# A hybrid attention and mixture-of-experts step on one core: experts chosen by ranks, the first job's tokens formed by one-hot products

## Chip, core and metric

The kernel runs on one core of a Trainium2 chip. The metric is the time of the whole program on the device, in microseconds (us); lower is better. A core has TensorE (PE, matrix products into eight PSUM banks), VectorE (DVE), ScalarE (ACT), GpSimd (POOL) and SyncE (SP), which here only issues DMAs. Engines meet by semaphores.

## What is computed

One layer over 512 prompt tokens and 64 sampled tokens (8 sequences of 8), width 1024, in fp32: attention in three branches and a pooling mixer, then `h = x + [a, m] @ w_out`, and on `rmsnorm(h)` a hierarchical mixture of 16 experts in 4 groups of 4. Each token takes its best group, and in it the two best experts:

```python
pg = softmax(x @ w_router_group)            # the best of 4 groups
g_val, g_idx = top_k(pg, 1)
le = (x @ w_router_expert)[experts of group g_idx]
e_val, e_idx = top_k(softmax(le), 2)
gate = g_val * e_val / sum(e_val)
y += gate_e * ((silu(x @ w_gate[e]) * (x @ w_up[e])) @ w_down[e])
```

The output is `h + y`, with the new key and value rows and pooling states beside it.

## The kernel before

The program is written by hand, engine by engine, in one block; each engine runs its list in order. The 576 tokens lie in five tiles, four of 128 rows and a last one of 64 (`ROWS`), and the residual `h` stays in `xh`. The stages are: input projection, compression of the cached keys, attention of the prompt, attention of the samples, and from about 366 us the output projection and the router.

**Router.** For each tile DVE adds the projection to `xh`, ACT sums the squares, DVE computes the inverse root `rstd` and writes `n2`, the normed row times `norm2_g` with its columns regrouped by eights (`by_chunk`), and ACT stores `n2` to `normed_rows` in HBM (`n_stored`). PE turns `xh` (L1265), DVE multiplies by `g2` (L2097), PE makes the logits (L1274), DVE scales them (L2117). For the last tile the normed row comes before the logits are read. Then DVE picks the group and two experts by a chain of maxima, comparisons and priorities (L2127 to L2153), each step waiting for the one before (`link`). PE counts with triangular matrices how many tokens before each one chose the same expert (`prefix`, L1313 and L1315). DVE derives for each token and choice a `job` and a `row` in it (L2164 to L2174) and writes one-hot matrices `picks` (L2182). PE turns them into `idx` (L1323), the token in each row of each job, and DVE copies it (L2190). Where PE would stand still, `keep_clock(k)` issues `WARM[k]` products whose result nobody reads (L1281, L1283).

**Jobs.** The experts' work is cut into `NJ` = 12 jobs of 128 rows: 96 rows of one expert, 32 of the fourth of its group of experts. POOL gathers the 128 token rows of a job from `normed_rows` by `idx` into `xg` (L2424), two buffers deep. PE turns them (L1337, `gathered_T`), ACT and DVE copy the halves into `xgT` (L1636, L2229), and PE runs gate, up and down products (L1353, `trio`) with 32-column stationary pieces. The transposes of job j+1 stand between the up and the down products of job j. Rows of a finished job go to HBM, those of the last are spread by a one-hot product. At the end rows are gathered, weighted and added. `crowded` reads `nmax`, the largest number of tokens of an expert, into a register of each engine, for a branch that is not taken here.

**Loads.** SP loads the 48 expert matrices of 2 MB into eight slots, in order; each load waits for the product that last used its slot (L836). The eighth goes over the buffers `n2`, and waits until all tiles are stored.

Of the kernel before, what the change touches and what calls it, by code (L numbers as in the profile page):

```python
# [42 lines left out]
WARM = (1, 2, 7, 3, 6)  # L43
# [123 lines left out]
def psum_plan():  # L167
# [103 lines left out]
    add("idx")  # L271
    add(("warm", 4))
# [3 lines left out]
def hybrid_step(nc, a, out, scratch):  # L276

    with ExitStack() as ctx:
# [91 lines left out]
        g2 = sb("g2", [P, KC])  # L370
        xnT = amT
# [93 lines left out]
        r16 = [view(kTs, 100 + i * 80, TILES, NE) for i in range(5)]  # L465
# [9 lines left out]
        in_fourth, base, late, job, row, beyond, which = (view(kTw, 330 + i * 10, 2, TILES) for i in range(7))  # L475
        r4 = [view(kTw, 400 + i * 20, TILES, NG) for i in range(4)]
# [22 lines left out]
        xg = [view(pflat, i * D, D) for i in range(2)]  # L499
        xgT = view(pflat, 2 * D, KC, P)  # L500
# [145 lines left out]
        def _(sp):  # L646
# [32 lines left out]
            sp.dma_start(g2[:, :], a["norm2_g"].rearrange("(k p) -> p k", p=P), allow_slow_non_contiguous=True).then_inc(ld_c1, 16)  # L679
            sp.dma_start(slc_bias[:, :], a["c_bands"]).then_inc(ld_c2, 16)  # L680
# [157 lines left out]
            for n, (e, m, _) in enumerate(matrix_loads()):  # L838
# [35 lines left out]
        def _(pe):  # L874
# [481 lines left out]
            def trio(j):  # L1356

                pe.wait_ge(xgt_ready, j * 2 + 2)
# [15 lines left out]
                for half in range(2):  # L1374
                    if j + 1 < NJ:
                        gathered_T((j + 1) % 2, (j + 1) // 2 * 16 + 16, [half])
# [5 lines left out]
                if j:  # L1382
                    pe.wait_ge(y_taken, j * 2)
                for half in range(2):
# [8 lines left out]
            gathered_T(0, 16, [0, 1])  # L1393
# [4 lines left out]
            pe.wait_ge(xgt_ready, 2 * NJ)  # L1398
# [51 lines left out]
        def _(sc):  # L1450
# [160 lines left out]
            for i in range(TILES):  # L1611
# [13 lines left out]
                sc.wait_ge(n_ready, i + 1)  # L1625
                sc.dma_start(scratch["n2"][i * P:i * P + n, :], n2[i % 2][0:n, :]).then_inc(n_stored[i % 2], 16)
# [11 lines left out]
            def trio(j):  # L1638
# [5 lines left out]
                if j + 1 < NJ:  # L1644
                    gathered(j + 2)
# [10 lines left out]
            gathered(1)  # L1656
# [23 lines left out]
        def _(ve):  # L1680
# [398 lines left out]
            link(ve.memset(logits, 0.0))  # L2079
            for i in range(TILES):  # L2080
# [19 lines left out]
                def normed_rows():  # L2100
# [3 lines left out]
                    link(ve.reciprocal(rstd[0:n, 1, i:i + 1], st[0:n, 16 + i:17 + i]))  # L2104
                    if i == 0:
                        ve.wait_ge(ld_g2, 16)
                    if i >= 2:
                        ve.wait_ge(n_stored[i % 2], 16 * (i // 2))
                    by_chunk = lambda row: row.rearrange("p (q k) -> p k q", k=KC)
                    ve.scalar_tensor_tensor(n2[i % 2][0:n, :].rearrange("p (k q) -> p k q", k=KC), by_chunk(xh[0:n, i, :]),  # L2110
# [3 lines left out]
                for stage in ((normed_rows, rows_of_router) if i < TILES - 1 else (rows_of_router, normed_rows)):  # L2114
                    stage()
# [11 lines left out]
            link(ve.tensor_reduce(r1[0], lg, X, ALU.max))  # L2127
            link(ve.tensor_tensor(r4[0], lg, over4(r1[0]), ALU.subtract))
            link(ve.tensor_tensor(r4[2], lg, over4(r1[0]), ALU.is_equal))
            link(ve.tensor_tensor(r4[2], r4[2], wide("prio4", NG), ALU.mult))  # L2130
            link(ve.tensor_reduce(r1[3], r4[2], X, ALU.max))
            link(ve.tensor_tensor(r4[3], r4[2], over4(r1[3]), ALU.is_equal))
            link(ve.tensor_scalar(r4[2], r4[3], -NEG, NEG, ALU.mult, ALU.add))
            ge = lambda x: x.rearrange("p t (g e) -> p t g e", g=NG)
            pen = spread(r4[2].rearrange("p t (g a) -> p t g a", a=1), 3, EPG)
# [455 lines left out]
```

## Time and profile before

| | us |
|---|---|
| median of 3 runs | 752.14 (752.06 to 753.49) |
| the profiled execution, its time | 753.13 |
| its span, first to last instruction | 751.4 |
| PE busy | 712.4 (95%) |
| DVE busy | 268.7 (36%) |
| ACT busy | 170.1 (23%) |
| POOL busy | 231.6 (31%) |

The span is what the trace's clock shows; the profiled execution's own time lies 1.73 us above it. Busy shares are means over stages with different limits, so the stretch around the router has to be read in the timeline.

### The profile page before, as it was taken

What the parts mean: (1) busy time and instruction counts of PE and PEld (TensorE: products, weight loads), DVE (VectorE), ACT (ScalarE), POOL (GpSimd) and SP (SyncE); (2) the same over time, 40 slices, a digit from 0 to 9 for tenths busy, and PEclk for the clock granted to TensorE, in tenths of its full rate; (3) what the DMA queues carried; (4) which work ended last, traced back from release to release, by engine and by line L of the source; (5) the groups of instructions that cost most, each with busy time, mean ns of one, the idle gap of its engine ahead of it and who ended that gap; (6) DMA issues with size and microseconds to landing.
All of it is one profiled execution on the core that took longest, in us unless ns stands there. A gap on an engine that the chain in (4) does not pass through costs nothing.

```text
span 751.4 us, 16367 instructions
## 1 busy us (share of the span) xinstructions
PE 712.4 (95%) x6460; PEld 401.1 (53%) x6460; DVE 268.7 (36%) x724; ACT 170.1 (23%) x366; POOL 231.6 (31%) x393
## 2 busy tenths in 40 slices
PE   6999999999989887988999998999999999999998
PEld 3555456865766554666645544454445555445542
DVE  1200054068678768566222366110011110001147
ACT  3100030248456644333010121000101000110100
POOL 2465156898575647444000001000000000000050
PEclk9999999999999899999999999999999999999999
DMA  9966523069801998467995065699999999999874
GB/s 300 262 174 230 173 50 71 20 198 226 228 20 40 323 310 266 134 180 211 241 415 223 29 265 182 241 321 358 399 419 425 419 422 420 424 413 420 352 270 137
DMA packets 81938, 191.79 MB, mean 255 GB/s; under 512 B 15798, under 2 KB 54982, under 8 KB 77373
## 3 DMA queue, kind: packets, MB, share of 16 engines
q1 hardware_dynamic: 67461, 150.63, 56.0%
q0 software_dynamic: 12160, 31.97, 13.0%
q10 hardware_dynamic: 2240, 8.13, 2.7%
q8 instruction: 52, 0.85, 0.4%
q14 instruction: 25, 0.20, 0.1%
HBM read 174.09 MB, written 16.70 MB: 254 GB/s over the span
## 4 chain that ended last, share of the span: by engine, by line
PE 53%; DVE 8%; issue 3%; DMA 2%; ACT 1%; SPq 1%; POOL 0%; DVEq 0%; POOLq 0%; ACTq 0%
PE bank L1353 31%; PE bank L1254 7%; PE bank L1337 2%; DVE arena L2011 2%; PE bank L1200 1%; PE bank L1445 1%; PE bank L1283 1%; PE bank L1274 1%; PE bank L1245 1%; DMA arena<-in_w_out 1%; DMA arena<-expert_rows,row_i 1%; DVE arena L2021 1%; DVE arena L2014 1%; PE bank L1379 1%; PE bank L1106 1%
## 5 line engine op out<-in xcount | busy, mean ns | idle before, releaser
L1353 PE MATMUL bank<-arena,proj 128*32 128x256 f32 (+1 forms) x2352 | 237.0, 479 | 1.3 <-DVE proj L2229 0.8
L1353 PEld LDWEIGHTS bank<-arena,proj 128*32 128x32 f32 x2352 | 103.3, 110 | 94.7 <-issue 76.3
L2424 POOL DMA_INDIRECT proj<-normed_rows,idx x12 | 11.4, 953 | 302.6 <-PE bank L1337 190.7
L909 PE MATMUL bank<-arena,amT 128*128 128x454 f32 x256 | 101.8, 556 | 1.1 <-DMA arena<-in_w_in 1.1
L2239 DVE TENSOR_TENSOR proj<-proj,bank 128x256 f32<-128x256 f32 x24 | 10.0, 421 | 208.1 <-PE bank L1353 208.1
L2334 POOL DMA_DIRECT2D arena<-in_cache_cmp_kv x128 | 68.6, 536 | 50.3 <-issue 42.6
L909 PEld LDWEIGHTS bank<-arena,amT 128*128 128x128 f32 x256 | 48.9, 194 | 50.0 <-issue 49.9
L2341 POOL DMA_DIRECT2D arena<-in_cache_slc_kv x96 | 51.5, 536 | 42.0 <-PE bank L1203 17.7
L1353 PE MATMUL bank<-amT,proj 128*32 128x512 f32 (+1 forms) x336 | 56.5, 532 | 0.0
L1353 PE MATMUL bank<-queries_and_bias,proj 128*32 128x512 f32 (+1 forms) x384 | 56.5, 486 | 0.0
L2354 POOL COPY arena<-arena 128x268 f32<-128x268 f32 x64 | 37.8, 647 | 27.9 <-PE bank L906 20.3
L1520 ACT ACTIVATE arena<-arena,st 128x512 f32<-128x512 f32 (+3 forms) x48 | 26.6, 554 | 35.5 <-DVE st L1915 35.5
L1650 ACT ACTIVATE proj<-bank 128x512 f32<-128x512 f32 x24 | 14.3, 598 | 82.5 <-PE bank L1353 82.5
L1353 PEld LDWEIGHTS bank<-queries_and_bias,proj 128*32 128x32 f32 x384 | 21.4, 110 | 17.3 <-issue 13.7
L1353 PEld LDWEIGHTS bank<-amT,proj 128*32 128x32 f32 x336 | 19.4, 110 | 19.1 <-issue 17.4
L1254 PE MATMUL bank<-arena,amT 128*128 128x512 f32 x64 | 29.0, 596 | 0.1
L1636 ACT ACTIVATE proj<-bank 128x512 f32<-128x512 f32 x12 | 7.2, 597 | 96.8 <-PE bank L1337 96.8
L1915 DVE CUSTOM_DVE_ANT_0 arena<-bank,queries_and_bias 128x512 f32<-128x512 f32 (+3 forms) x48 | 21.6, 488 | 13.3 <-PE bank L1063 12.4
L2435 POOL DMA_INDIRECT arena<-expert_rows,row_i x8 | 8.0, 998 | 56.9 <-DMA expert_rows<-proj 54.8
L1643 ACT ACTIVATE proj<-bank 128x512 f32<-128x512 f32 x12 | 7.2, 598 | 77.4 <-PE bank L1353 77.4
L1106 PE MATMUL bank<-mats,arena 128*128 128x128 f32 x120 | 19.4, 296 | 4.6 <-ACT proj L1535 4.4
L2354 POOL COPY xh<-arena 128x268 f32<-128x268 f32 x32 | 22.5, 749 | 4.0 <-PE bank L926 3.9
(358 smaller groups left out, 1011.9 us busy)
## 6 DMA issues: line engine op xcount, KB each, us to landing
arena<-in_w_up SPq DMA_DIRECT2D x13, 2048.0 KB, 16.5
arena<-in_w_down SPq DMA_DIRECT2D x13, 2048.0 KB, 16.6
arena<-in_w_gate SPq DMA_DIRECT2D x10, 2048.0 KB, 17.1
arena<-in_cache_cmp_kv POOLq DMA_DIRECT2D x128, 64.0 KB, 2.5
arena<-in_cache_cmp_kv SPq DMA_DIRECT2D x128, 64.0 KB, 2.2
amT<-in_w_gate SPq DMA_DIRECT2D x3, 2048.0 KB, 12.8
queries_and_bias<-in_w_gate SPq DMA_DIRECT2D x3, 2048.0 KB, 11.6
expert_rows<-proj ACTq DMA_DIRECT2D x11, 512.0 KB, 9.7
```

The source lines that it names most:

```text
L909: last = pe.matmul(ps(("in", c, i))[0:n, 0:WC], xnT[:, k, i * P:i * P + n], w_in[c % 2][:, k, :], start=k == 0, stop=k == KC - 1)
L1106: last = pe.transpose(ps(("p_T", u, k))[:, c * P:(c + 1) * P], pS[u % 4][:, k, c * P:(c + 1) * P], ident)
L1254: last = pe.matmul(ps(("h", i, half))[0:n, :], amT[:, k, i * P:i * P + n], out_matrix(k, half), start=k == 0, stop=k == KC - 1)
L1337: last = pe.transpose(BX[half][:, k * P:(k + 1) * P], xg[slot][:, c:c + P], ident)
L1353: ins = pe.matmul(dst[part, :], rows[:, part], own if q < TRIO else shared, start=start, stop=stop)
L1520: sc.activation(z, z, ACT.Exp, bias=st[:, m:m + 1], scale=-1.0, accum_out=st[:, d:d + 1]).then_inc(p_e, 1)
L1650: sc.activation(ytok[:, half * 512:(half + 1) * 512], BY[half][:, :], ACT.Copy).then_inc(y_taken, 1)
L1915: read(ve.tensor_tensor_reduce(pS[u % 4][:, k, 0:n], ps(("p_s", u, k))[:, 0:n], dist[:, SEQ - n:SEQ], -SLOPES[g + G * k], 3e38, ALU.add, A ...
L2011: read(ve.scalar_tensor_tensor(z3, lanes, table["row_slope"], ps(name)[:, :].rearrange("p (n l) -> p n l", l=64), ALU.mult, ALU.add), name)
L2334: po.dma_start(sides[:, b // 4, b % 4 * PAGES + k, :], src).then_inc(ld_last, 16)
L2341: po.dma_start(pages[b % 4][:, k, first * P:(first + count) * P], src)\
L2354: po.tensor_copy(chunk_out(r, d), chunk_in(d)).then_inc(regrouped, 1)
```

## The change

Three things change. First, the experts are chosen by ranks: within the groups, and within each group of four experts, every value is compared with every other (`beats4`, `beats16`; an earlier one wins a tie), the comparisons are summed to ranks, and ranks 0 and 1 of the group of rank 0 are the choice. The maxima that the gates need are taken later. Second, the rows of job 0 are not fetched. DVE writes for each tile `spot`, a one-hot matrix from token to row of job 0, scaled by `rstd`, and PE multiplies `xh` (read by `by_chunk`, stationary) with it; the result is the turned rows in two banks, and ACT and DVE multiply by `g2_rows` (a new load of `norm2_g`) into `xgT`. POOL fetches jobs 1 to 11. Third, the normed rows of the last tile are written after `idx`, into `xg[0]`, and stored later. `WARM` is shorter.

```diff
-WARM = (1, 2, 7, 3, 6)
+WARM = (1, 2, 4, 2)
...
+    for half in range(2):
+        add(("rows", half), bank=2 + half)
+    add("idx", bank=5)
...
+        def normed(i):
+
+            return n2[i % 2] if i < TILES - 1 else xg[0]
...
+            sp.dma_start(g2_rows[:, :], a["norm2_g"].rearrange("(p k) -> p k", p=P)).then_inc(ld_c1, 16)
...
-                    sp.wait_ge(n_stored[0], 48)
+                    sp.wait_ge(n_stored[0], 32)
...
+            for half in range(2):
+                opened(pe, ("rows", half))
+            for i in range(TILES):
+                n = ROWS[i]
+                pe.wait_ge(picks_ready, i + 1)
+                by_chunk = xh[0:n, i, :].rearrange("p (q k) -> p k q", k=KC)
+                for half in range(2):
+                    for k in range(4):
+                        last = pe.matmul(ps(("rows", half))[:, k * P:(k + 1) * P], by_chunk[:, 4 * half + k, :], spot[0:n, i, :],
+                                         start=i == k == 0, stop=i == TILES - 1 and k == 3)
+                    if i == TILES - 1:
+                        written(last, ("rows", half))
             opened(pe, "idx")
             for n in range(2 * TILES):
                 i, k = n // 2, n % 2
-                pe.wait_ge(picks_ready, n + 1)
+                pe.wait_ge(picks_ready, TILES + n + 1)
                 last = pe.matmul(ps("idx")[:, 0:NJ], picks[:, n, :], tok_at[:, k, i, :], start=n == 0, stop=n == 2 * TILES - 1)
             written(last, "idx")
-            keep_clock(4)
...
-                pe.wait_ge(free[b], used[b])
+                if b != plan["idx"][0]:
+                    pe.wait_ge(free[b], used[b])
...
-                pe.wait_ge(xgt_ready, j * 2 + 2)
+                if j:
+                    pe.wait_ge(xgt_ready, 2 * j)
...
-            gathered_T(0, 16, [0, 1])
...
+                if i < TILES - 1:
+                    sc.wait_ge(n_ready, i + 1)
+                    sc.dma_start(scratch["n2"][i * P:i * P + n, :], normed(i)[0:n, :]).then_inc(n_stored[i % 2], 16)
+            filled(sc, ("rows", 0))
+            for k in range(4):
+                last = sc.activation(xgT[:, k, :], ps(("rows", 0))[:, k * P:(k + 1) * P], ACT.Copy, scale=g2_rows[:, k:k + 1])
+            read(last, ("rows", 0))
+            sc.wait_ge(n_ready, TILES)
+            sc.dma_start(scratch["n2"][SEQ:NT, :], normed(TILES - 1)[0:NS, :]).then_inc(n_stored[0], 16)
...
+            link(ve.memset(rstd[:, 1, :], 0.0))
...
+                if i < TILES - 1:
+                    inverse_root()
+                    normed_rows(i)
+                    rows_of_router()
+                else:
+                    rows_of_router()
+                    inverse_root()
...
+            link(ve.memset(chosen[:, TILES, :], 0.0))
...
+            groups = lg.rearrange("p t (a g) -> p t a g", a=1)
+            experts = ge(le)
+
+            for j in range(NG):
+                for low, high, better in ((0, j + 1, ALU.is_gt), (j + 1, NG, ALU.is_ge)):
+                    if low < high:
+                        one = spread(groups[:, :, :, j:j + 1], 3, high - low)
+                        ve.tensor_tensor(beats4[:, :, low:high, j], one[:, :, 0, :], lg[:, :, low:high], better)
+                        one = spread(experts[:, :, :, j:j + 1], 3, high - low)
+                        last = ve.tensor_tensor(beats16.rearrange("p (t g) i j -> p t g i j", g=NG)[:, :, :, low:high, j], one,
+                                                experts[:, :, :, low:high], better)
+            link(last)
+            ve.tensor_reduce(rank4, beats4, X, ALU.add)
+            link(ve.tensor_reduce(rank16.rearrange("p t (g e) -> p (t g) e", g=NG), beats16, X, ALU.add))
+            link(ve.scalar_tensor_tensor(in_group, rank4, 0.0, over4(table["valid"]), ALU.is_equal, ALU.mult))
+            its_group = spread(in_group.rearrange("p t (g a) -> p t g a", a=1), 3, EPG)
+            ve.scalar_tensor_tensor(ge(chosen[:, 0:TILES, :]), ge(rank16), 1.5, its_group, ALU.is_lt, ALU.mult).then_inc(oh_ready, 1)
+            for k in range(2):
+                last = ve.scalar_tensor_tensor(ge(hot[:, k]), ge(rank16), float(k), its_group, ALU.is_equal, ALU.mult)
+            link(last)
...
+            roots = spread(rstd[:, 1, :].rearrange("p (a i) -> p a i", a=1), 1, 2)
+            link(ve.scalar_tensor_tensor(in_first, job, 0.0, roots, ALU.is_equal, ALU.mult))
+            for i in range(TILES):
+                for k in range(2):
+                    last = ve.tensor_scalar((spot[:, i, :], picks[:, i, :])[k], table["row"], row[:, k, i:i + 1], in_first[:, k, i:i + 1],
+                                            ALU.is_equal, ALU.mult)
+                link(last)
+                ve.tensor_tensor(spot[:, i, :], spot[:, i, :], picks[:, i, :], ALU.add).then_inc(picks_ready, 1)
...
+            ve.wait_ge(picks_ready, TILES)
...
+            filled(ve, ("rows", 1))
+            read(ve.tensor_tensor(xgT[:, 4:8, :], ps(("rows", 1))[:, :].rearrange("p (k t) -> p k t", k=4), bc(g2_rows[:, 4:8], P), ALU.mult),
+                 ("rows", 1))
...
+            normed_rows(TILES - 1)
+
+            link(ve.tensor_reduce(r1[0], lg, X, ALU.max))
+            link(ve.tensor_tensor(r4[0], lg, over4(r1[0]), ALU.subtract))
+            link(ve.tensor_tensor(pair16, hot, over_k(le), ALU.mult))
+            link(ve.tensor_reduce(top, pair16, X, ALU.add))
+            ve.tensor_tensor(r1[6], top[:, 1, :], top[:, 0, :], ALU.subtract).then_inc(r_exp_in, 1)
...
-            gathered(1)
...
-            for j in range(NJ):
-                if j >= 2:
-                    po.wait_ge(xt_full, j - 1)
+            for j in range(1, NJ):
+                if j >= 3:
+                    po.wait_ge(xt_full, j - 2)
```

In the same diff, the counts of `gathered`, `gathered_T`, `xt_full` and `xgt_ready` are lowered by one job, job 0's down products wait for `idx` to be copied, and the old selection (L2127 to L2154, `first_max`) is deleted.

On PE, between the last logits and job 0, before (`mats` as the only source is filler, `kTw,mats` the counting, `proj` with 12 columns is `idx`, `mats,proj` the transposes of fetched rows):

```order
L1283 MATMUL bank<-mats 128x512 x7
L1313 MATMUL bank<-kTw,mats 128x96
...
L1281 MATMUL bank<-mats 128x128
L1283 MATMUL bank<-mats 128x512 x3
L1323 MATMUL bank<-proj 128x12 x10
L1281 MATMUL bank<-mats 128x128
L1283 MATMUL bank<-mats 128x512 x6
L640 TENSOR_LOAD nmax
L640 ISA x2
L1337 MATMUL bank<-mats,proj 128x128 x8
L1353 MATMUL bank<-arena,proj 32x512 x32
```

And after:

```order
L1297 MATMUL bank<-mats 128x512 x4
L1327 MATMUL bank<-kTw,mats 128x96
...
L1295 MATMUL bank<-mats 128x128
L1297 MATMUL bank<-mats 128x512 x2
L1341 MATMUL bank<-proj,xh 128x128 x40
L1349 MATMUL bank<-proj 128x12 x10
L653 TENSOR_LOAD nmax
L653 ISA x2
L1379 MATMUL bank<-arena,proj 32x512 x32
```

The forty products stand between the shortened filler and `idx`; the filler behind `idx` and the eight transposes are gone, and the register read follows `idx`.

On DVE, from the end of `row` to behind the copy of `idx`, before (`kTw` holds the small values, `proj` the one-hots):

```order
L2174 SCALAR_TENSOR_TENSOR kTw<-kTw 128x10
L2176 TENSOR_TENSOR proj<-small,kTw 128x120
L2178 TENSOR_TENSOR proj<-proj,small 128x60 x2
L2182 TENSOR_SCALAR proj<-small,kTw 128x128 x10
L2184 TENSOR_REDUCE kTw<-bank 128x1
L2186 CAST nmax<-kTw 1x1
L2189 COPY kTw<-bank 128x1
L2190 CAST idx<-bank 128x12
L2194 TENSOR_TENSOR kTw<-kTs,small 128x160
```

And after (L2148 is the line of `normed_rows`):

```order
L2211 SCALAR_TENSOR_TENSOR kTw<-kTw,rstd 128x10
L2214 TENSOR_SCALAR proj<-small,kTw 128x128 x2
L2217 TENSOR_TENSOR proj<-proj 128x128
...
L2221 TENSOR_TENSOR proj<-proj,small 128x60 x2
L2226 TENSOR_SCALAR proj<-small,kTw 128x128 x10
L2228 TENSOR_REDUCE kTw<-bank 128x1
L2230 CAST nmax<-kTw 1x1
L2233 TENSOR_TENSOR proj<-bank,g_rows 128x512
L2236 COPY kTw<-bank 128x1
L2237 CAST idx<-bank 128x12
L2148 SCALAR_TENSOR_TENSOR proj<-xh,rstd,proj 64x1024
L2242 TENSOR_REDUCE kTw<-kTs 128x5
```

The scaled one-hots of five tiles come ahead of everything that serves `idx`, the copy out of the `rows` bank ahead of the copy of `idx`, and the normed rows of the last tile behind it.

## Rows read from the trace of the kernel before

**Rows 1.** Chain that ended last, expert jobs: start us, us, what.

```profile
467.34 13.98 PE bank L1353 x192
...
482.78 20.80 PE bank L1353 x256
```

**Rows 2.** Waits of SP's DMA queue: total us, times, longest.

```profile
SPq L836 <- PE bank L1353: 230.7, 31, 23.9
```

**Rows 3.** The same chain, just before job 0.

```profile
459.35 5.15 PE bank L1283 x12
464.51 0.96 issue
465.46 1.10 PE bank L1337 x8
```

**Rows 4.** Timeline around the selection: start us, us, engine, line, operation, names, count.

```profile
444.40 2.07 DVE L2110 SCALAR_TENSOR_TENSOR queries_and_bias<-xh,rstd,proj 64x1024 f32<-64x1024 f32 x1
...
445.16 6.17 PE L1283 MATMUL bank<-mats 128*128 128x512 f32 x14
...
446.39 0.22 DVE L2117 TENSOR_SCALAR kTs<-bank,rstd 64x20 f32<-64x20 f32 x1
...
446.74 0.18 DVE L2127 TENSOR_REDUCE kTw<-kTs 128x5 f32<-128x20 f32 x1
...
451.93 0.24 DVE L2153 TENSOR_TENSOR kTw<-kTw,small 128x80 f32<-128x80 f32 x1
```

**Rows 5.** Timeline from the counting products to the end of DVE's list.

```profile
452.23 0.46 PE L1313 MATMUL bank<-kTw,mats 128*128 128x96 f32 x2 [0.89 <-DVE kTw L2153]
...
453.85 0.32 DVE L2164 TENSOR_TENSOR kTw<-kTs,bank 128x160 f32<-128x160 f32 x1 [0.24 <-PE bank L1315]
...
454.56 0.17 DVE L2167 TENSOR_SCALAR kTw<-kTw 128x10 f32<-128x10 f32 x1
...
454.64 0.17 DVE L2168 TENSOR_SCALAR kTw<-kTw 128x10 f32<-128x10 f32 x1
...
455.49 0.16 DVE L2174 SCALAR_TENSOR_TENSOR kTw<-kTw 128x10 f32<-128x10 f32 x1
...
456.39 2.05 DVE L2182 TENSOR_SCALAR proj<-small,kTw 128x128 f32<-128x128 f32 x10
...
456.82 2.37 PE L1323 MATMUL bank<-proj 128*128 128x12 f32 x20 [0.35 <-DVE proj L2182]
...
459.43 0.17 DVE L2190 CAST idx<-bank 128x12 int32<-128x12 f32 x1
...
465.19 0.23 DVE L2222 TENSOR_SCALAR kTw<-small,kTw 128x5 f32<-128x5 f32 x1
```

**Rows 6.** Timeline of PE in the pooling products of 128 x 128 by 128 columns.

```profile
130.31 0.39 PE L945 MATMUL bank<-queries_and_bias,proj 128*128 128x128 f32 x2
130.54 0.39 PE L947 MATMUL bank<-queries_and_bias,proj 128*128 128x128 f32 x2
```

**Rows 7.** Groups of DVE instructions by shape: busy us, mean ns.

```profile
L1975 DVE COPY xh<-arena 128x268 f32<-128x268 f32 x16 | 10.7, 708 | 1.2 <-POOL arena L2359 1.1
...
L1967 DVE COPY proj<-bank 128x512 f32<-128x512 f32 x9 | 6.1, 685 | 0.6 <-PE bank L1106 0.6
...
L2266 DVE TENSOR_SCALAR proj<-small,kTw 128x128 f32<-128x128 f32 x5 | 1.4, 346 | 0.0
```

**Rows 8.** DMA issues, 440 to 470 us: KB, us to landing; then all twelve fetches.

```profile
normed_rows<-queries_and_bias ACTq DMA_DIRECT2D x1, 256.0 KB, 3.7
proj<-normed_rows,idx POOLq DMA_INDIRECT x3, 4.4
...
DMA to landing us min/median/max: 4.3/8.5/11.1
```

**Rows 9.** Page, section 5: busy us, mean ns, idle before.

```profile
L909 PE MATMUL bank<-arena,amT 128*128 128x454 f32 x256 | 101.8, 556 | 1.1 <-DMA arena<-in_w_in 1.1
```

**Rows 10.** Windows: us, busy us (count) of PE, PEld, DVE, ACT, POOL, clock, DMA share, GB/s.

```profile
450.00:456.00 6.00, 5.11 (x23) 2.73 (x21) 5.08 (x26) 0.32 (x2) 0.00 (x0) 1.00 0.80 279
```

More of the change, by code:

```diff
@@ L370, in hybrid_step @@
         g2 = sb("g2", [P, KC])
+        g2_rows = sb("g2_rows", [P, KC])
         xnT = amT
@@ L464, in hybrid_step @@
         w_r = sb("w_r", [P, KC, NG + NE])
-        r16 = [view(kTs, 100 + i * 80, TILES, NE) for i in range(5)]
+        rank16 = view(kTs, 100, TILES, NE)
+        hot = view(kTs, 100 + 2 * 80, 2, TILES * NE).rearrange("p k (i e) -> p k i e", e=NE)
+        beats16 = view(QB[:, :, :].rearrange("p a b -> p (a b)"), 0, TILES * NG, EPG, EPG)
+        beats4 = view(QB[:, :, :].rearrange("p a b -> p (a b)"), TILES * NE * EPG, TILES, NG, NG)
+        rank4, in_group = (view(kTs, 500 + i * 20, TILES, NG) for i in range(2))
+        top = view(kTs, 540, 2, TILES)
         pair16 = view(kTw, 96, 2, TILES * NE).rearrange("p k (i e) -> p k i e", e=NE)
@@ L475, in hybrid_step @@
         in_fourth, base, late, job, row, beyond, which = (view(kTw, 330 + i * 10, 2, TILES) for i in range(7))
+        in_first = view(kTw, 510, 2, TILES)
         r4 = [view(kTw, 400 + i * 20, TILES, NG) for i in range(4)]
@@ L1375, in trio @@
                     if j + 1 < NJ:
-                        gathered_T((j + 1) % 2, (j + 1) // 2 * 16 + 16, [half])
+                        gathered_T((j + 1) % 2, (j + 2) // 2 * 16, [half])
                     pe.wait_ge(he_ready, 2 * j + half + 1)
@@ L1383, in trio @@
                     pe.wait_ge(y_taken, j * 2)
+                else:
+                    taken(pe, "idx")
                 for half in range(2):
@@ L1644, in trio @@
                 if j + 1 < NJ:
-                    gathered(j + 2)
+                    gathered(j + 1)
                 if j:
@@ L2098, in rows_of_router, with inverse_root @@
                              ("nT", i, half))
-                def normed_rows():
+                def inverse_root():
                     ve.wait_ge(h_sq, i + 1)
@@ L2126, in _ @@
             wide = lambda name, n: spread(table[name].rearrange("p (a n) -> p a n", a=1), 1, TILES)
[L2127 to L2132, printed above, removed]
@@ L2145, in _ @@
-            flat = lambda x: x.rearrange("p a b -> p (a b)")
-            first_max(r16[0], r1[4], r16[2])
-            link(ve.scalar_tensor_tensor(flat(r16[1]), flat(r16[2]), NEG, flat(r16[0]), ALU.mult, ALU.add))
-            first_max(r16[1], r1[6], r16[3])
-            hot = view(kTs, 100 + 2 * 80, 2, TILES * NE).rearrange("p k (i e) -> p k i e", e=NE)
-            link(ve.memset(chosen[:, TILES, :], 0.0))
-            link(ve.tensor_tensor(chosen[:, 0:TILES, :], r16[2], r16[3], ALU.add))
@@ L2153, in _ @@
-            ve.tensor_tensor(chosen[:, 0:TILES, :], chosen[:, 0:TILES, :], over16(table["valid"]), ALU.mult).then_inc(oh_ready, 1)
-            ve.tensor_tensor(r1[6], r1[6], r1[4], ALU.subtract).then_inc(r_exp_in, 1)
+            link(ve.memset(chosen[:, TILES, :], 0.0))
+            ge = lambda x: x.rearrange("p t (g e) -> p t g e", g=NG)
+            groups = lg.rearrange("p t (a g) -> p t a g", a=1)
[8 more added lines that the diff above has]
+                                                experts[:, :, :, low:high], better)
@@ L2155, in _ @@
+            for k in range(2):
+                last = ve.scalar_tensor_tensor(ge(hot[:, k]), ge(rank16), float(k), its_group, ALU.is_equal, ALU.mult)
+            link(last)
             over_k = lambda x: spread(x.rearrange("p (a i) e -> p a i e", a=1), 1, 2)
-            link(ve.tensor_tensor(hot, hot, over_k(over16(table["valid"])), ALU.mult))
             link(ve.tensor_tensor(pair16, hot, over_k(wide("seat", NE)), ALU.mult))
@@ L2247, in trio @@
                 if j + 1 < NJ:
-                    gathered(j + 2)
+                    gathered(j + 1)
             def gathered_rows(i):
@@ L2476, in _ @@
             po.wait_ge(st_pool, 16 * (1 + DB))
-N_C1 = 16 * (1 + 3 + 2 + 4 + 2 + 1 + 1)
+N_C1 = 16 * (1 + 3 + 2 + 4 + 2 + 1 + 2)
 N_OUT = 3 + 3 + DB
```

27 lines of the change are left out of this document (7 added, 20 removed).

## The prediction

> **What bounds the kernel now.** I read the page first (TensorE, PE, is busy 95% of the span), then the chain of work that ended last, the waits of the DMA queue, and the timeline around the router. From 467.34 us on, twelve expert jobs run on PE: the gate and up products of job 0 take 13.98 us, and each later piece of 20.8 us is followed by 1.5 us of transposes, 22.33 us a job, with no gap that a transfer causes [rows 1]. The loads of expert matrices wait for PE's products, 230.7 us in all, so the weights follow PE and not the other way round [rows 2]. Whatever moves the start of job 0 (call it S, 467.34 now) moves the end by as much, as long as nothing in job 0 starts to wait. The prediction is therefore about S.
>
> Before S stands a serial stretch. VectorE (DVE) picks experts, PE counts them, DVE makes one-hot matrices, PE turns these into `idx`, GpSimd (POOL) fetches rows, PE transposes them. At its end PE is not waiting for the fetch: it runs its own filler products until 464.50, then 0.96 us of its queue reading `nmax` into a register, then the transposes [rows 3], 1.9 us up to S with their copies.
>
> **The router on DVE.** Now `normed_rows` of the last tile (2.07 us) stands between DVE and the last logits, though PE had ended them at 445.1: they are read at 446.39 [rows 4]. After the change they are read at about 445.1, a gain of 1.3 us. The selection starts 0.35 us after that read and its one-hots are ready at 452.17, so it takes 5.4 us [rows 4]. The new one is 14 comparisons that do not wait for one another, then two sums, and two products. Unlinked small operations start 0.08 us apart [rows 5], and one of 128 elements takes 0.205 us of the pace (ten in 2.05 us) [rows 5], so about 0.07 us plus 1.05 ns per element. 14 x 0.07 + 400 elements x 1.05 ns = 1.4 us, the wait behind them 0.1, the clearing of `chosen` 0.1, the sums 0.15 and 0.5 (320 elements), the products 0.2 and 0.25: 2.7 us. The one-hots are ready at 445.1 + 0.35 + 2.7 = 448.2, 4.0 us earlier. PE's filler before it is cut from 7 to 4 products. Seven took 6.17 us [rows 4], 0.86 each, so four end at 448.7. The filler now ends last by 0.4 us, and hides an error of that size in the 2.7. The counting products start at 448.6 instead of 452.23; DVE reads them 1.62 us later, at 450.2, and has `row` and `job` at 452.0 (455.65 now, from 453.85 + 1.80) [rows 5]. Up to here 3.6 us are gained.
>
> **Job 0 without a fetch.** DVE adds `in_first` (0.2 us), then for each tile two scaled one-hots and their sum. The scaled one-hot exists now, in another place: 0.346 us each [rows 7], at a pace like that of the plain ones. Per tile 0.2 + 0.35 + 0.03 for the link + 0.28 for the sum, of which the next tile hides a little: 0.85 us, the first ready at 453.2. PE then multiplies: 5 tiles x 8 chunks, 40 products of 128 x 128 with 128 columns, two records each. The nearest rows are the pool products of the same shape: one starts each 0.2225 us (130.31 to 130.54) [rows 6]. 40 x 0.2225 = 8.9 us, so PE sets the pace (1.78 us per tile against 0.85 on DVE), and the `rows` banks are full at 453.2 + 8.9 + 0.2 = 462.3. Behind them in PE's order stand the ten `idx` products, 2.37 us [rows 5]; they end at 464.5. DVE's one-hots for these (2.05 us [rows 5], and 0.75 us for `tok_at`) are done near 459.3 and `nmax` near 459.9, behind PE. The copies out of the `rows` banks take 0.69 us on DVE [rows 7] and about 1 us on ScalarE (ACT), whose half is full 0.9 us earlier; both are over at 463.1, under the `idx` products. The 6 filler products, the 8 transposes and their 0.70 us copy are gone. What is left is the register read: 0.96 us now, when PE's last product must have ended first. After the change it follows `idx` directly and waits only for the copies, so it costs between 0 (read while the products drain) and 0.96. I take half: S = 464.5 + 0.5 = 465.0, 2.3 us earlier than 467.34. The gain of 3.6 us shrinks because the path from `row` to S grows from 11.7 to 13.0 us.
>
> **What is late next.** Every one of POOL's fetches now waits for the last tile's store, and that is written later: `idx` is read at 464.9 on DVE, `normed_rows` ends at 467.0, ACT issues the store, which lands after 3.7 us at 470.7, and POOL issues job 1's fetch at 471.0. It lands after 4.4 us with idle queues: 475.4 [rows 8]. PE asks for it when job 0's up products are done, S + 13.98 = 479.0. The cover is 3.6 us; with the median landing of all fetches, 8.5 us, it is gone and 0.5 us over [rows 8]. Behind `normed_rows` DVE has five new operations (1.2 us) and its old list, 459.60 to 465.42 now [rows 5], done at about 474.0, and a register read like PE's, 475.0; its first hidden product is due at S + 10.5 = 475.5. Close, but PE needs that product only after S + 14. ACT's exponentials with their table load fit before the first Silu at S + 7. The load of `w_up` into `queries_and_bias` no longer waits for the last store; it was not waited for.
>
> **At nothing:** the extra small load of `g2_rows` moves SyncE's later issues by one issue. The input products waited for a load for 1.1 us in all, once, at their first, ahead of this issue [rows 9]; page loads run far ahead of their use. Clearing `rstd` falls into DVE's wait for the first projection.
>
> **Sum** on the profiled execution: span 751.4 - 2.3 = 749.1, its time 753.13 - 2.3 = 750.8. The median of the three runs is 0.99 us under that profiled time, 752.14 - 2.3 = **749.8 us**. Its own range is 748.9 to 751.0 (the register read at either end, 0.4 us on the comparisons). A measurement of this kernel can tell about 0.2%, 1.5 us, from no change.
>
> **Rival 1: the stationary operand is read with gaps (slower).** `by_chunk` takes every eighth float of `xh`, 32 bytes apart, and no PE row before does that. DVE has such rows: 268 elements read with gaps take 708 ns, and 512 read densely out of a bank 685 ns [rows 7], so an element costs twice, about 2.1 ns. If PE's weight loads double their pace of 0.111 us, 80 of them cost 8.9 us more and the time is 758.7. If they cost DVE's 2.1 ns for each of 128 columns, 0.267 us each, it is 12.5 us more, 762.3. It decides from 2.3 us on, that is at 0.14 us per load. Against it speaks only that the loads overlap the streams (two in flight) and that another engine's reads set no price for PE. I give it 0.31, two thirds of that at the doubled pace.
>
> [...]
>
> **Rival 2: job 1's tokens come late.** With the slowest landing, 11.1 us [rows 8], the fetch is there at 482.1, PE waits 3.1 us in job 0 and the time is 752.9; with 8.5 us it is 750.3. For it: job 1's load of the down matrix starts at S + 7 and shares the queues. Against it: only one such load is then under way. 0.12, at about 751.5.
>
> **Rival 3: the new DVE work gains nothing.** If each of the 14 comparisons costs what a linked one does (0.24 us), they take 3.4 us instead of 1.4, beyond the filler's cover of 0.4: 1.6 us, and with slower scaled one-hots 2.3 us, 752.1. 0.08.
>
> [...] 0.04 for this and the unforeseen.
>
> **Numbers.** Forecast 0.45, rival 1 0.31, rival 2 0.12, rival 3 0.08, rest 0.04. Faster: 0.45 + half of rival 2 + a little = 0.52; same 0.14; slower 0.34. The range must take in the doubled pace of rival 1, and leaves out its upper price: 748.9 to 759.3.
>
> **What would show it.** In the changed profile: the last logits read near 445.1; the one-hots 3 us later; forty products at L1341 in 8.9 us (17.8 or more under rival 1, with weight loads clearly over 0.19 us each); job 0's first product at 465.0; PE's wait for job 1's transposes at about 479 at most some tenths; jobs still 22.33 us apart. The prediction is wrong if the forty products take over 11 us, or if PE waits for the fetch.

## The result, and the profile after

The change made the kernel slower: 764.77 us (764.3 to 767.76, 4 runs) against 752.82 us (752.06 to 755.21, 4 runs) of the kernel before beside it, a ratio of 1.0174 [1.0154, 1.0193]. The forecast was 749.8, with 759.3 as its upper end. The profiled execution took 764.3 us, with a span of 762.6. Everything ahead of the change's place ran 1.6 us earlier in this execution than in the one of before (the last logits end at 443.46, not 445.07), so times around the router are compared below as distances from that end, called L.

The chain of work that ended last, in the changed kernel: start us, us, what.

```profile
443.72 3.44 PE bank L1297 x8
...
447.35 1.06 PE bank L1329 x10
...
451.62 19.59 PE bank L1341 x80
471.21 4.38 PE bank L1349 x20
475.58 16.51 PE bank L1379 x192
...
493.56 20.80 PE bank L1379 x256
...
515.84 20.85 PE bank L1379 x256
```

The reader is to see the forty products (80 records) at 19.59 us, the `idx` products at 4.38 instead of 2.37 [rows 5], and job 0's first piece at 16.51 instead of 13.98 [rows 1]. Job 0 starts at L + 32.1 (before L + 22.3). Behind it the jobs are 22.33 us apart as before.

DVE's timeline in the same execution (start us, us, engine, line, operation, names, shapes, count, idle before):

```profile
443.57 0.23 DVE L2160 TENSOR_SCALAR kTs<-bank,rstd 64x20 f32<-64x20 f32 x1 [0.82 <-PE bank L1288]
...
445.35 0.30 DVE L2181 TENSOR_TENSOR QB<-kTs 128x80 f32<-128x80 f32 x1
...
446.56 0.24 DVE L2188 SCALAR_TENSOR_TENSOR kTw<-kTs 128x80 f32<-128x80 f32 x1
...
450.54 0.60 DVE L2214 TENSOR_SCALAR proj<-small,kTw 128x128 f32<-128x128 f32 x2
451.18 0.29 DVE L2217 TENSOR_TENSOR proj<-proj 128x128 f32<-128x128 f32 x1
451.39 0.60 DVE L2214 TENSOR_SCALAR proj<-small,kTw 128x128 f32<-128x128 f32 x2
```

The logits are read 0.1 us after L, the one-hots are ready at 446.80, L + 3.3 (predicted 3.1), and a tile's scaled one-hots take 0.85 us (predicted 0.85). The first of the forty products starts at L + 8.2 (predicted 8.1). All terms up to there held.

What a single one of the forty costs: the instructions of line L1341 in the changed kernel, their duration in ns (min/median/max).

```profile
L1341 PEld LDWEIGHTS bank<-proj,xh x80: 309/335/340, 451.6 to 470.6; 128*128 128x128 f32 x64, 64*128 64x128 f32 x16
L1341 PE MATMUL bank<-proj,xh x80: 364/402/502, 451.6 to 470.8; 128*128 128x128 f32 x64, 64*128 64x128 f32 x16
```

And the windows of the changed kernel (columns as in [rows 10]; the clock is the third number from the end):

```profile
453.00:454.00 1.00, 1.00 (x6) 1.00 (x6) 0.97 (x5) 0.00 (x0) 0.00 (x0) 0.75 0.09 16
454.00:455.00 1.00, 1.00 (x6) 1.00 (x6) 0.97 (x4) 0.00 (x0) 0.00 (x0) 0.50 0.00 0
...
457.00:458.00 1.00, 1.00 (x6) 1.00 (x5) 0.73 (x5) 0.00 (x0) 0.00 (x0) 1.00 0.00 0
...
462.00:468.00 6.00, 6.00 (x26) 5.88 (x26) 0.00 (x0) 0.00 (x0) 0.00 (x0) 1.00 0.00 0
...
474.00:480.00 6.00, 6.00 (x32) 2.67 (x35) 4.02 (x10) 1.19 (x1) 0.00 (x0) 0.50 0.10 23
```

The clock was not at 1.00 throughout this stretch, as it was before (1.00 from 444 to 486 us): it was at 0.50 from 453.5 to 456.9 and again from 470.6 to 480.8. In what follows such a stretch is called a spell. Each window counts every record that touches it, so that six in one microsecond are about four that start in it; the 6 us at 462 show 26. A weight load starts every 0.24 us in the first spell and every 0.24 us behind it, so their pace did not follow the clock. In the second spell `idx` (4.38 us for 2.37) and job 0 (16.51 for 13.98) did slow down.

### The profile page after: what moved, and what is told of

Read it like the earlier page. It is cut to its first block, busy times and chain, and to the rows that moved or that the text cites. A ratio compares the mean times of both kernels' runs of the same rounds, so it can differ in the third digit from the quotient of the medians.

```text
span 762.6 us, 16494 instructions
## 1 busy us (share of the span) xinstructions
PE 725.3 (95%) x6511; PEld 416.7 (55%) x6511; DVE 271.4 (36%) x743; ACT 170.7 (22%) x369; POOL 230.3 (30%) x392
## 4 chain that ended last, share of the span: by engine, by line
PE 58%; DVE 6%; issue 2%; ACT 1%; DVEq 0%; ACTq 0%
PE bank L1379 33%; PE bank L1268 7%; PE bank L1341 3%; PE bank L1214 2%; DVE arena L2045 1%; PE bank L1363 1%; PE bank L1473 1%; PE bank L1288 1%; PE bank L1259 1%; DVE arena L2055 1%; PE bank L1297 1%; DVE arena L2048 1%; PE bank L1406 1%; PE bank L1090 1%; PE bank L1120 1%
## 5 line engine op out<-in xcount | busy, mean ns | idle before, releaser
L1379 PE MATMUL bank<-arena,proj 128*32 128x256 f32 (+1 forms) x2352 | 239.6, 484 | 0.2
L1379 PE MATMUL bank<-amT,proj 128*32 128x512 f32 (+1 forms) x336 | 58.2, 537 | 0.0
L1379 PE MATMUL bank<-queries_and_bias,proj 128*32 128x512 f32 (+1 forms) x384 | 58.2, 501 | 0.0
## 6 DMA issues: line engine op xcount, KB each, us to landing
arena<-in_w_up SPq DMA_DIRECT2D x13, 2048.0 KB, 17.6
```

Source lines behind the costliest of these rows:

```text
L1379: ins = pe.matmul(dst[part, :], rows[:, part], own if q < TRIO else shared, start=start, stop=stop)
```

## The experiments

Theory A was rival 1: the stationary operand read 32 bytes apart sets the pace of the products. Theory B: the clock sets it. Experiments 1, 2, 5 and 6 ran on one chip, beside 752.24 us of the kernel before (19 runs); L is taken anew from each profile.

**1. Dense columns (r1_dense).** Features of job 0 are mixed up by it.

```diff
-                by_chunk = xh[0:n, i, :].rearrange("p (q k) -> p k q", k=KC)
+                by_chunk = xh[0:n, i, :].rearrange("p (k q) -> p k q", k=KC)
```

> The changed kernel, but the forty products for job 0 read their stationary operand densely (128 neighbouring columns of the residual) instead of every eighth. This mixes up the order of job 0's input features, so its output is not the reference's; sizes and counts are the same. Theory A (the gaps in the stationary read make each weight load slow, and the clock falls because PE then computes too little): forty products in 8.9 us instead of 19.6, clock 1.00 throughout, idx products 2.4 us instead of 4.4, job 0's gate and up 14.0 us instead of 16.5; 15.1 us less than 764.8, so 749.7 us. Theory B (the clock falls because filler products were taken out, and the slow products are a result of that): the products stay above 15 us, the clock still falls, the time stays above 758 us.

Measured: 753.83 us (10 runs), ratio 1.0015 [0.9996, 1.0034], span 751.0. Its chain, the instructions of L1341, and windows:

```profile
452.81 9.36 PE bank L1341 x80
462.18 2.33 PE bank L1349 x20
464.51 15.61 PE bank L1379 x192
```

```profile
L1341 PEld LDWEIGHTS bank<-proj,xh x80: 183/192/192, 452.8 to 461.8; 128*128 128x128 f32 x64, 64*128 64x128 f32 x16
```

```profile
463.00:464.00 1.00, 1.00 (x11) 1.00 (x11) 0.00 (x0) 0.00 (x0) 0.00 (x0) 1.00 0.00 0
...
465.00:466.00 1.00, 1.00 (x12) 0.36 (x8) 0.94 (x1) 0.00 (x0) 0.00 (x0) 0.50 0.00 0
```

That one word is worth 10.2 us of products and 143 ns of each weight load. Job 0 starts at 464.51, L + 19.85 (predicted 19.9), with some luck: even dense, the products take 9.36 us and not 8.9, and the register read, put at 0.5, costs nothing. Yet the kernel is no faster than before. The clock falls to 0.50 at 464.8 for 3.4 us, and job 0's first piece takes 15.61 us instead of 13.98. Of the gain of 2.4 us that leaves 0.8, and in the profiled execution the last stage took just that back: a store of experts' rows and the fetch behind it took 3.79 + 6.03 us, against 2.62 + 6.40 before. These terms put the ratio at 0.9989 without the last stage and at 1.000 with it; what the median has beyond that isn't explained. Theory A holds for the products; its "job 0 14.0" failed.

**2. A ladder of steps (r2_ladder).** Tile 0 is read with step 1, tiles 1 to 4 with 2, 3, 4 and 8 floats (so other features).

```diff
+                step = (1, 2, 3, 4, 8)[i]
+                by_chunk = [xh[0:n, i, c:c + step * (P - 1) + 1:step] for c in range(KC)]
...
```

> The changed kernel, but the five tiles of the forty products read the stationary operand with steps of 1, 2, 3, 4 and 8 elements (4, 8, 12, 16, 32 bytes), 16 records each; the output is not the reference's, since other columns of the residual are read. [...] Theory A, in a form where any gap costs: 0.24 us from step 2 on. Theory B: all five tiles alike, at the pace that the clock sets.

Measured: 761.23 us (one run), products 14.56 us. Weight loads of the five tiles, from windows inside each, in tile order:

```profile
L1342 PEld LDWEIGHTS bank<-proj,xh x16: 186/192/192, 452.9 to 454.5; 128*128 128x128 f32 x16
...
L1342 PEld LDWEIGHTS bank<-proj,xh x15: 192/197/198, 454.5 to 456.2; 128*128 128x128 f32 x15
...
L1342 PEld LDWEIGHTS bank<-proj,xh x15: 198/261/264, 456.3 to 458.6; 128*128 128x128 f32 x15
...
L1342 PEld LDWEIGHTS bank<-proj,xh x13: 329/330/330, 459.8 to 462.6; 128*128 128x128 f32 x13
...
L1342 PEld LDWEIGHTS bank<-proj,xh x9: 309/331/333, 462.6 to 464.7; 64*128 64x128 f32 x7, 128*128 128x128 f32 x2
```

Medians 192, 197, 261, 330, 331 ns: elements 8 bytes apart cost next to nothing more than neighbours, 12 bytes apart half of the extra, 16 bytes all of it, 32 bytes no more than 16. So the price does not grow from 16 to 32 bytes, and not any gap costs: the form of Theory A that put 0.24 us from step 2 on failed at step 2, at 197 ns a load. Why 12 bytes cost about half of it was not shown.

**3. The gaps on the moving side (r7_moving).** The same ladder with the two operands exchanged; on a second, slower chip (before: 759.76 us there).

```diff
-...by_chunk[4 * half + k], spot[0:n, i, :],
+...spot[0:n, i, :], by_chunk[4 * half + k],
```

> The changed kernel with the operands of the forty products exchanged: the one-hot matrix is stationary and read densely, the residual moves, with steps of 1, 2, 3, 4 and 8 elements for the five tiles; the output is not the reference's (rows and features are exchanged, other columns read). If gaps cost on any read of PE: matmul records longer at steps 3, 4 and 8, about 0.18 and 0.24 us apart, weight loads 0.19 us throughout. If they cost only where weights are loaded: 0.11 us apart at every step, 80 records in 9.4 us.

Measured: 766.56 us (one run), the products 14.16 us against 14.56. At step 4 the streams are long and the weight loads nearly short:

```profile
L1342 PE MATMUL bank<-xh,proj x14: 340/405/408, 458.8 to 461.6; 128*128 128x128 f32 x14
L1342 PEld LDWEIGHTS bank<-xh,proj x13: 196/208/208, 458.9 to 461.6; 128*128 128x128 f32 x13
```

The gap costs about as much when the operand moves (405 ns, against 275 at step 1); exchanging the operands is no way out.

**4. The first gap filled (r8_gap_filled).** One more filler product before the first tile, on the second chip.

```diff
-WARM = (1, 2, 4, 2)
+WARM = (1, 2, 4, 3)
```

> The changed kernel as it is, with one more filler product (3 instead of 2) in the 1.35 us gap ahead of the forty products; computes what the reference does. If the gap sets off the first fall of the clock (453 to 457 us): no fall there, the forty products up to 1 us shorter than 19.6 us; the second fall, from 471 us on, stays, job 0's gate and up still 16 us or more. If the slow weight loads alone let the clock fall: both falls stay. Time within 1.5 us of 764.8 either way.

Measured: 772.23 us (one run), 12.5 us above before on that chip.

```profile
452.79 19.58 PE bank L1341 x80
472.36 4.37 PE bank L1349 x20
476.73 15.60 PE bank L1379 x192
```

The first spell is gone (clock 1.00 until 469.9) and the products take 19.58 us instead of 19.59. Theory B is refuted for them. The second spell stays, 10.2 us long, and it begins after PE has been busy without a break for 17 us.

**5. Every feature in plain order (r4_plain).** Dense columns and the real output: the weights of gate and up are loaded as `(k p)` too, in pieces of 2 KB instead of 16 KB, and the normed rows and `g2_rows` follow.

```diff
-                    src = (a["w_gate"], a["w_up"])[m][e].rearrange("(p k) f -> p k f", p=P)
+                    src = (a["w_gate"], a["w_up"])[m][e].rearrange("(k p) f -> p k f", p=P)
...
```

> The changed kernel with the features of every job in plain order: the residual, the normed rows and the g2 factors are read densely, and the gate and up matrices are loaded so that partition p holds rows p, 128 + p, and so on (eight pieces of 2 KB per partition instead of one of 16 KB). Computes what the reference does. Theory A: as the dense one, and normed_rows takes 1.3 us a tile instead of 2.1; if the smaller pieces cost the transfers nothing, 749.7 us or some tenths less. Rival: the transfers run at about 420 GB/s in the jobs, so smaller pieces make PE wait for weights and jobs take over 22.33 us; each 0.1 us per job costs 1.2 us.

Measured: 764.4 us (4 runs), ratio 1.0152 [1.0104, 1.02]. Products 9.36 us, job 0 at L + 19.8, but later the chain shows PE waiting for matrices:

```profile
592.55 5.09 PE bank L1379 x45
597.65 21.71 DMA arena<-in_w_down
...
670.01 20.24 DMA arena<-in_w_down
```

The 21.71 and 20.24 us are whole transfers; PE itself stood still for 4.7 us in two waits for down matrices. The median load into `arena` of an up matrix takes 22.1 us, against 17.6 in the changed kernel. The regrouping by eights is what lets these loads come in long pieces, so loaded in this way the plain order costs more than it gives.

**6. The ranks alone (r3_ranks)**, in the kernel before, fetch kept.

```diff
-WARM = (1, 2, 7, 3, 6)
+WARM = (1, 2, 4, 3, 6)
```

with the diff's selection and, behind `idx`, its maxima for the gates.

> The kernel before with the selection by ranks alone (filler before the counting products 4 instead of 7, nothing else of the change). If the ranks save what the changed trace shows, one-hots 3.3 us after the last logits end instead of 7.1 with 1.3 of these for the normed rows that stay here: start of job 0 and end 2.4 to 2.6 us earlier, 750.3 us. Rival: the fetch or the register read takes the gain back, time within 1 us of 752.8.

Measured: 751.91 us (10 runs), ratio 0.9995 [0.9975, 1.0016], on the first chip.

```profile
464.27 0.55 DVEq L645
...
465.18 0.70 DVE proj L2231
465.92 15.47 PE bank L1358 x192
```

The transposes start at L + 17.8, 2.6 us earlier than before, but DVE's list is now longer than the fetch: it reads its register at 464.27 and copies job 0's half at 465.18, 0.8 us after PE. Job 0 starts at L + 20.5, 1.8 us earlier than before, and then loses 1.5 us to the lower clock.

**7. DVE's copy first (r5_copy_first).** As 6, with that copy ahead of the gates; on the second chip.

```diff
+            ve.wait_ge(xt_full, 1)
+            ve.tensor_copy(xgT[:, 4:8, :], EXPERT_BANKS[2][1][:, :].rearrange("p (k t) -> p k t", k=4)).then_inc(xgt_ready, 1)
             ve.wait_ge(r_exp, 1)
```

> The ranks-only kernel, with DVE's copy of job 0's turned rows moved ahead of the twelve small operations for the gates, so that DVE's longer list does not hold it up by 0.8 us. If the gap of 1.6 us on PE ahead of job 0 was what let the clock fall in the ranks-only kernel: gap 0.8 us, clock 1.00, job 0's gate and up 14.0 us instead of 15.5, start of job 0 19.7 us after the last logits end (22.3 before), span 2.6 us under before's, 750.2 us. Rival: the clock falls nevertheless (fewer filler products ahead), job 0 takes 15.5 us, and the time is 751.5 us.

Measured: 759.05 us (12 runs), ratio 0.999 [0.9974, 1.0006].

```profile
456.87 6.85 PE bank L1288 x12
463.72 0.96 issue
464.68 1.10 PE bank L1342 x8
```

The copy no longer waits, and job 0 takes 13.98, but the spell lay inside the filler this time, which took 6.85 us instead of 5.15 and set the start: L + 21.4.

**8. Filler behind the dense products (r6_dense_fill).** Experiment 1 with three filler products behind `idx`; second chip.

```diff
+            keep_clock(4)
```

> The dense kernel (job 0's features in the wrong order, output not the reference's) with three filler products of 512 columns behind the idx products. Theory 1 (the clock fell in the dense kernel because the stretch of 128- and 12-column products gives PE little to do, and filler right behind it holds the clock): clock 1.00, job 0's gate and up 14.0 us instead of 15.6, its start 2.7 us later. Theory 2 (the fall is set off by the stretch itself and comes even if filler follows): the filler falls into the slow spell, clock under 1 at 465 to 468 us, job 0 nearly whole after it.

Measured: 763.94 us (one run). The filler took 4.29 us, with the clock at 0.50 from 464.6 to 468.0, where three products at 1.00 take 2.6 (estimated from six in 5.15 [rows 3]), and job 0 took 13.98. So a spell came with filler there as it did with job 0 in experiment 1, and slowed what ran in it: here the filler, there job 0 (15.61 us).

**9 to 12. Where the filler stands.** Experiment 7 with other counts: `WARM` (1, 2, 5, 3, 6), (1, 2, 4, 4, 6), (1, 2, 5, 4, 6) and (1, 2, 4, 3, 4). All four on a chip where the kernel before took 752.72 us (30 runs). Theory I: idle stretches of PE ahead of a spell set it off. Theory N: they do not, and it comes all the same.

> The kernel before with the ranks and with DVE's copy of job 0 first, and five filler products instead of four ahead of the counting, so that PE hardly stands still there (0.90 us idle in the run with four). [...] Theory N (idle stretches are not the cause): a spell of about 3.5 us somewhere between 452 and 470, and with it 1.6 us back: ratio 0.999 to 1.0.

> As the run with DVE's copy first, but four filler products instead of three between the counting and the idx products, where PE stood still for 0.35 us. They end about 0.5 us after the one-hots are ready, so everything behind is 0.5 us later. Theory I, if this gap were the one that matters: no spell, ratio about 0.998. Theory N: the spell stays, near 457, filler 6.85 us again, ratio about 1.000.

> Both gaps filled: five filler products ahead of the counting and four ahead of the idx products. Theory I: no spell at all, clock 1.00 from 444 to 486, job 0 13.98 us, start about 20.6 us after the last logits, ratio about 0.998. Theory N: a spell of about 3.5 us all the same, ratio 1.000 or above.

> As the run with DVE's copy first, but four instead of six filler products behind the idx products, so that PE waits for the fetched rows (issued at 457.5, 4.4 us to landing) and not for its filler, with about 1.5 us of standing still. Theory I (standing still sets a spell off): the spell falls later, into job 0, whose first piece takes 15.5 us; start about 19.9 us after the last logits; ratio about 0.999. Theory N (the products before set it off, and the idle time is no matter): a spell at 457 to 460 as with six, which now costs little, since the filler then still ends before the rows are there: job 0 13.98 us, start about 20.0 us after the logits, ratio about 0.997.

| run | us | ratio | job 0 starts | its first piece |
|---|---|---|---|---|
| r9_fill_first | 750.79 | 0.9971 [0.9949, 0.9993] | L + 21.4 | 13.98 |
| r10_fill_second | 751.37 | 0.9984 [0.9964, 1.0004] | L + 20.0 | 15.68 |
| r11_fill_both | 751.06 | 0.9985 [0.9969, 1.0001] | L + 20.0 | 15.68 |
| r12_fill_less | 748.53 | 0.9947 [0.9927, 0.9966] | L + 19.7 | 13.98 |

All four showed a spell: in the filler at 456 to 459 (r9), in job 0 at 465.1 to 468.5 (r10, r11). Theory I's forecast failed: with both gaps filled, PE stood still nowhere between the last logits and the end of the last filler, and the clock fell all the same. That run alone doesn't clear every pause of PE, since the register read (0.96 us) and the wait for the copy (0.78) still stand right ahead of its spell; but in experiment 1 the clock fell after 12 us without any pause, and in experiment 4 after 17. In r12, the fastest, the spell lay on the filler too. Its windows, the fetch of job 0's rows, and its chain:

```profile
454.00:455.00 1.00, 1.00 (x11) 1.00 (x11) 0.43 (x4) 0.00 (x0) 0.00 (x0) 1.00 0.99 426
...
456.00:457.00 1.00, 1.00 (x2) 0.34 (x1) 0.93 (x4) 0.17 (x2) 0.71 (x1) 0.50 0.00 0
```

```profile
455.68 1.03 POOL L2428 DMA_INDIRECT proj<-normed_rows,idx  x1 [109.10 <-DVEq L2189]
```

```profile
455.09 5.13 PE bank L1288 x8
460.22 0.96 issue
461.18 1.10 PE bank L1342 x8
...
463.05 13.98 PE bank L1358 x192
```

The spell was not free there. Four filler products took 5.13 us, what six take at full clock (5.15), and with the register read they still ended last: the rows, issued at 455.68 and 4.4 us on the way, were there at about 460.1, the transposes started at 461.18. Of the 1.7 us that the spell added, 1.1 reached the start of job 0. What the two dropped products bought is that the spell cost no more.

**13. The shorter filler alone (r13_filler_alone)**, in the kernel before, to tell its part in the gain from that of the ranks; on a chip where before took 759.72 us (23 runs).

```diff
-WARM = (1, 2, 7, 3, 6)
+WARM = (1, 2, 7, 3, 4)
```

> The kernel before with nothing changed but the filler behind the idx products, four instead of six. Control for the version with ranks and four (ratio 0.9947). The filler then ends 1.7 us earlier, at 462.8 instead of 464.5, the register read at 463.7, and the transposes wait for the fetched rows (issued at 459.94, 4.4 us to landing, so 464.3 at the latest) instead of starting at 465.46. Theory F (the gain of that version came from this cut): S about 1.1 to 1.7 us earlier, ratio 0.998 or less, and the ranks only the rest. [...]

Measured: 758.9 us (12 runs), ratio 0.9991 [0.9972, 1.0009]. The transposes start at 464.00, when the rows are there (L + 19.4, before L + 20.4), but DVE copies at 465.91, behind its list, and job 0 starts at L + 22.0, 0.2 us earlier than before, with no spell. Theory F is refuted by this start: the cut alone gives nothing (the interval of the times alone would not exclude its 0.998). But here DVE's list holds the copy up. No run has the cut and the copy first without the ranks; from the transposes at L + 19.4 and the 1.9 us from there to job 0 in the kernel before, job 0 would start at L + 21.3, an estimate. So up to 1.0 of r12's 2.6 us may be had without the ranks.

**14. Two filler products (r14_fill_least).** Experiment 7 with `WARM` (1, 2, 4, 3, 2), beside 13.

> The version with ranks, DVE's copy of job 0 first and two filler products behind idx instead of four. [...] Theory C (the spell comes at about the same time whatever follows, and costs what PE does then): filler over by 458, the transposes start when the rows land, near 460.1, one us earlier than with four, job 0 13.98 us; ratio about 0.993. Theory M (the spell needs running products and moves on when they are fewer): it lands in job 0, 15.5 us, ratio about 0.997.

Measured: 759.33 us (12 runs), ratio 0.9992 [0.9972, 1.0012].

```profile
457.61 4.32 DMA proj<-normed_rows,idx
...
461.98 1.98 PE bank L1342 x8
...
464.73 15.66 PE bank L1358 x192
```

PE stood still for 3.2 us and waited for the fetch. The clock was at 0.50 from 461.3 to 468.2: transposes 1.98 us instead of 1.10, job 0 15.66. Theory M's loss came about, but not by its reason: the spell began while PE stood still, and lasted 6.8 us instead of 3.4. In these single profiles four products did better than two and better than six.

## Why the prediction was wrong

**The step that failed** is "The nearest rows are the pool products of the same shape: one starts each 0.2225 us ... 40 x 0.2225 = 8.9 us". These rows [rows 6] read their stationary operand densely. With 32 bytes between elements a weight load took 335 ns instead of 192, and the forty took 19.59 us, 10.7 over the term (0.5 of these the dense products miss too, at 9.36). By the prediction's own sign, over 11 us, it was wrong. It had this as rival 1 at 0.31, and the mechanism is the one it described. The measured 10.7 lies midway between its two prices, 8.9 (the doubled pace, to which it gave two thirds and at which it cut its range) and 12.5. With that term alone and the free register read the sum is 749.8 + 10.7 - 0.5 = 760.0, already above the range. DVE's rows [rows 7], two times the cost per element with gaps, were a better guide than the hope that overlap hides it. Experiments 1, 2 and 4 show it: the word removed, the step varied, the clock kept.

**The second term was not in the sum at all.** The clock stands at 1.00 in the rows [rows 10], where PE has gaps too (5.11 of 6.00 us busy), and a fall was given 0.04 together with everything unforeseen. The first spell didn't slow the new products at all (19.59 us with it, 19.58 without it in experiment 4). The second spell had a price: in the changed profile it cost 2.0 us in `idx` and 2.5 us in job 0; with dense columns 1.6 us. The sum with both terms: 749.8 + 10.7 + 2.0 - 0.5 (the register read proved free) + 2.5 = 764.5, where 764.77 was measured.

**What held.** The logits read without `normed_rows` ahead, the ranks (one-hots 0.2 us later than predicted), the filler ending last, `row` and `job`, and the scaled one-hots: the first product started within 0.1 us of its predicted distance from L. The copies of the banks ended under `idx`. The register read cost nothing: job 0's products start when those of `idx` end (475.59 and 475.58). Everything behind job 0 kept its 22.33 us.

**Rival 2** did not come about: job 1's fetch was issued at 481.99 and no product waited for it; job 0 had itself moved to 475.6. Whether it would be late with S at 465 is answered by experiment 1: there the pieces of jobs 0 and 1 stand 1.46 us apart (480.12 and 481.58), the transposes alone. **Rival 3** is refuted by the one-hots at L + 3.3.

**Where the gain went.** The ranks and the earlier read of the logits did give 2.4 us at S (experiment 1), and 1.8 with DVE's copy held up (experiment 6). In both, 1.5 to 1.6 us were lost again to a spell at 0.50 in job 0. In r12_fill_less the spell cost 1.1 us and the rest stayed: S 2.6 us earlier relative to L, which is 0.9965 of the time before, at the edge of the measured [0.9927, 0.9966]. The mean clock of each run tells where more can come from: the five of its ten runs at 0.998 took 748.43 in the median, the sixteen of before at 0.998 took 752.1, 3.7 us more, and 2.6 + 1.1 is 3.7. That version has the ranks, the fetch, DVE's copy first and four filler products, and beats both kernels.

**Open:** what sets a spell off. Experiments 7, 12 and 14 have the same instructions on PE up to the second filler product behind `idx`; in the profiles of 7 and 12 the clock fell at L + 12, in that of 14 not until L + 16. Experiment 6 has the same on PE up to job 0 as 7, and its clock fell at L + 20. So the place isn't given by PE's list alone. Something may have been settled long before: of the eleven profiles with a fall at L + 12 or L + 20, the eight at L + 20 also have a spell near 212 us, and the three at L + 12 (experiments 7, 9 and 12) don't (the falls in the changed kernel and in experiments 4 and 14 lie elsewhere). That may be chance of the execution rather than the work of `WARM`. Each is one profiled execution, and how often r12's spell falls on the filler isn't known. Nor are spells a thing of the change: the kernel before has them too, from 212.2 to 215.6 and from 246.3 to 253.1 us, only none around the router. That the earlier selection brings one there is argued, not shown: all variants with it have one and the two profiles without it (before and experiment 13) have none. The mean clocks fit for most: 0.998 in 16 of 30 runs of before, and in 4 of 29 of r9, r10 and r11, but in 5 of 10 of r12.

## What to carry to other kernels

Price a PE product by rows that read its operands with the same spacing: here a view that takes every fourth or eighth float made a 128-column load 1.7 times as long (330 and 335 ns for 192) and a stream 1.5 times (405 ns for 275 at every fourth), and forty products in a row 2.1 times (19.59 us for 9.36 at every eighth), and the denser neighbour [rows 6] misled. When a serial stretch in front of PE's long work is shortened, look at the granted clock behind it before counting the gain. Filler that ends last costs what it takes at the lower clock: in r12_fill_less four products took 5.13 us with the clock at 0.50 for 3.4 of these, what six took at 1.00 (5.15). How much of it to leave has to be measured: here four products did better than six, and better than two. A layout that makes one operand dense may be paid for by the loads of the other: in r4_plain the products took 9.36 us, but the median load of an up matrix 22.1 us for 17.6.

## What the runs showed of the hardware

- Weight loads of 128 fp32 columns took 192, 197, 261, 330 and 331 ns at steps of 4, 8, 12, 16 and 32 bytes; the moving side took 405 ns for 275 at 16 bytes.
- With 32-byte steps the pace was the same at both levels of the clock: a load each 0.24 us at 0.50 and at 1.00 (453.5 to 456.9 us of the changed kernel and behind it), and all forty products took 19.59 us with a spell in them and 19.58 without (r8_gap_filled).
- Spells at 0.50 began after 12 us (r1_dense) and 17 us (r8_gap_filled) in which PE was never idle. Around the router they were 3.4 us long in most profiles, 6.8 in r14_fill_least, and 10.2, begun within the products with gaps, in all four profiles that have these (the changed kernel, r2_ladder, r7_moving, r8_gap_filled).
- The kernel before shows spells too, from 212.2 to 215.6 and from 246.3 to 253.1 us.
- A register read on PE (0.96 us behind filler) was wholly hidden behind the twenty `idx` records when nothing else had to be waited for (the changed kernel and r1_dense).
